# A bidirectional state-space scan taken over pairs of tokens, both directions in one step

## What is computed

```python
def ssm_direction(u_c, lam_re, lam_im, log_step, b_re, b_im, c_re, c_im, reverse):
    lam = lax.complex(lam_re, lam_im)
    step = jnp.exp(log_step)[:, None]
    lam_bar = jnp.exp(lam * step)
    b_bar = ((lam_bar - 1.0) / lam)[:, :, None] * b
    bu = jnp.einsum('blgh,gph->blgp', u_c, b_bar)
    a = jnp.broadcast_to(lam_bar, (1, bu.shape[1]) + lam_bar.shape)
    _, states = lax.associative_scan(_scan_combine, (a, bu), reverse=reverse, axis=1)
    return jnp.real(jnp.einsum('blgp,ghp->blgh', states, c))

y = u32 * d_skip + ssm_direction(forward) + ssm_direction(reverse)
y = jax.nn.gelu(y)
y = y * jax.nn.sigmoid(y @ w_glu + b_glu)
return rmsnorm(y, g_out)
```

## Time and profile before

| | |
|---|---|
| median of three runs | 1778.12 us (1773.86 to 1780.32) |
| the profiled execution | 1774.65 us, of which its span is 1772.8 us |
| PE busy | 1634.9 us, 92% of the span |
| DVE busy | 1386.7 us, 78% |
| ACT busy | 1069.4 us, 60% |
| POOL busy | 260.5 us, 15% |

### The profile page before, as it was taken

How to read it: one execution, slowest core, us unless ns; L and a number is a source line. 1 busy time by engine, 2 the same in 40 slices (tenths; PEclk the granted TensorE clock), 3 DMA queues, 4 the chain that set the end, 5 groups by cost and what they waited for, 6 DMA issues and landing times.

```text
span 1772.8 us, 21337 instructions
## 1 busy us (share of the span) xinstructions
PE 1634.9 (92%) x6878; PEld 1231.4 (69%) x6879; DVE 1386.7 (78%) x1421; ACT 1069.4 (60%) x1252; POOL 260.5 (15%) x202
## 2 busy tenths in 40 slices
PE   6978888999798888799999999999999999999994
PEld 5634346888673434588788788788788787887883
DVE  5699956444378996688888888888888888888883
ACT  4466624433245763477677677677676676776772
POOL 0666620000046655000000000000000000000000
PEclk9976699999997578899999999999999999999998
DMA  9210006455321000399899899899899798998980
GB/s 380 95 48 19 6 0 231 173 189 190 142 112 78 1 24 1 134 351 373 317 370 374 308 369 377 302 367 376 309 377 373 304 374 334 344 375 315 366 334 37
DMA packets 56927, 423.22 MB, mean 239 GB/s; under 512 B 6449, under 2 KB 6449, under 8 KB 7217
## 3 DMA queue, kind: packets, MB, share of 16 engines
q1 hardware_dynamic: 56016, 417.40, 61.6%
q0 software_dynamic: 864, 5.24, 0.7%
HBM read 421.57 MB, written 1.05 MB: 238 GB/s over the span
## 4 chain that ended last, share of the span: by engine, by line
PE 81%; DVE 9%; ACT 5%; issue 3%; POOL 1%; DVEq 0%; DMA 0%; ACTq 0%; SPq 0%; POOLq 0%
PE ps L1225 42%; PE ps L1213 20%; PE ps L1068 5%; PE ps L1082 2%; PE ps L1096 2%; PE ps L1317 2%; PE ps L1179 2%; PE ps L1164 2%; PE ps L1193 2%; DVE work L769 1%; DVE wl L822 1%; PE ps L1152 1%; PE ps L1140 1%; ACT wh L449 1%; DVE work L722 1%
## 5 line engine op out<-in xcount | busy, mean ns | idle before, releaser
L822 DVE TENSOR_TENSOR wl<-raw,wh 128x2048 fp32r<-128x2048 f32 x369 | 834.8, 2290 | 134.9 <-ACT wh L449 123.2
L449 ACT ACTIVATE wh<-raw 128x2048 fp32r<-128x2048 f32 x369 | 693.4, 1914 | 0.0
L1225 PE MATMUL ps<-wh,xh 128*128 128x512 f32 x1072 | 431.4, 402 | 9.4 <-DVE xl L909 5.5
L1225 PE MATMUL ps<-wl,xh 128*128 128x512 f32 x1072 | 419.5, 391 | 0.0
L1225 PE MATMUL ps<-wh,xl 128*128 128x512 f32 x1072 | 418.7, 391 | 0.0
L1225 PEld LDWEIGHTS ps<-wh,xh 128*128 128x128 f32 x1072 | 201.9, 188 | 50.0 <-issue 9.3
L1225 PEld LDWEIGHTS ps<-wl,xh 128*128 128x128 f32 x1072 | 201.7, 188 | 42.8
L1225 PEld LDWEIGHTS ps<-wh,xl 128*128 128x128 f32 x1072 | 202.3, 189 | 40.1 <-issue 1.7
L457 ACT ACTIVATE hidh<-ps 128x256 fp32r<-128x256 f32 (+1 forms) x123 | 49.5, 402 | 271.2 <-PE ps L1193 271.2
L1213 PE MATMUL ps<-wh,hidh 128*128 128x512 f32 x536 | 165.8, 391 | 5.8 <-DVE hidl L829 5.8
L1213 PE MATMUL ps<-wh,hidl 128*128 128x512 f32 x536 | 165.1, 389 | 0.0
(11 more groups left out here) (196 smaller groups left out, 1692.4 us busy)
## 6 DMA issues: line engine op xcount, KB each, us to landing
raw<-wffn SPq DMA_DIRECT2D x369, 1024.0 KB, 5.2
mixw<-wmix SPq DMA_DIRECT2D x12, 2048.0 KB, 8.1
bw<-bmat POOLq DMA_DIRECT2D x2, 1024.0 KB, 10.2
cat<-cmat POOLq DMA_DIRECT2D x2, 1024.0 KB, 14.9
qk<-wglu SPq DMA_DIRECT2D x2, 1024.0 KB, 4.8
X<-x_in SPq DMA_DIRECT2D x1, 1024.0 KB, 4.9
ybuf<-rows POOLq DMA_DIRECT2D x2, 512.0 KB, 3.5
y_out<-hn SPq DMA_DIRECT2D x2, 512.0 KB, 2.7
```

What stands on the lines that cost most here:

```text
L449: nc.scalar.activation(wh[:, slot], raw[:, slot], ACT.Copy).then_inc(s["hi_done"], 1)
L822: tt(wl[:, slot], raw[:, slot], wh[:, slot].bitcast(F32), ALU.subtract).then_inc(s["lo_done"], 1)
L1225: ins = mm(ps[:, b], x2[:, fx, t * P:(t + 1) * P], w2[:, slot, f * 512:(f + 1) * 512], start=(fx == 0 and i == 0), stop=(fx == KT - 1 and ...
```

## The change

The tokens are laid out by parity: partition p holds tokens 2p and 2p+1, so the 256 columns of a transposed tile are the 128 even tokens and then the 128 odd ones. The constants for distances in the attention follow that order. For the scan, tokens are taken in pairs. The recurrence over pairs has the squared transition (decay `small[:, 16]`, which is the exponential of twice the exponent; angles from twice the angle), 128 elements long instead of 256. Its input is b u(2k) and b u(2k+1), one of them multiplied by the transition, in one product of 64 rows. One step does the forward and the reverse direction of a pair of groups, 128 columns each, so there are 16 steps. Token outputs that the pair state doesn't hold are given by a local term: a 128x128 matrix `loc` for each two steps, which also holds the skip `d_skip`, times the pair of tokens.

What that takes on each engine:

- SP: `spread_u` copies `u` from `uT` into the pair layouts `ush` and `usw`, 8 + 8 DMAs in a layer between buffers of the core (each 32 partitions, 4 rows of 128 elements). `gather_y` copies the output of each of the four feature tiles back to the order of `glu`, 8 DMAs each (32 partitions of 128 elements). The last of them stands behind the loads of two 1 MB pieces, in whose buffers (`LENT`) the scan's temporaries now lie.
- POOL's queue: the matrix for b is 2 MB instead of 1 MB, that for c 2 MB instead of 1 MB, and `dmat` of 0.5 MB is new. The three operations of a step keep their shape; there are 16 of each in a layer instead of 32.
- DVE before step 0: `scalars` is rearranged (35 operations instead of 30); `turn_b` is new (12 operations of 128x512 elements); `fold_c` has six of 128x2048.
- PE before step 0: 32 transposes of 128x128 for b, which ACT empties in eight copies of 128x512. PE waits with `bu(0)` for them and for `ush`.
- DVE in a step: `fracs`, `rotate_in` and `add_in` keep their shape, the scan is four instructions of 128 elements instead of two of 256. Once in a layer, four operations of 32x256 add into `loc`.
- ACT in a step: four angle instructions of 128 elements instead of two of 256; the rest keeps its shape.
- PE in a step: `bu` is four products of 128 columns instead of two of 256, `outputs` too, and in every second step a product with `loc` of 128 columns. `local` is 32 products of 64 columns in a layer.
- The attention's stages stand two steps apart instead of four, and the six projections in steps 0 to 3. Half of `attention_out` now comes after the last scan.

```diff
-ZQKV_AT = (0, 1, 2, 4, 6, 8)
-HEAD_AT = [9 + 4 * h for h in range(HEADS)]
+ZQKV_AT = (0, 0, 1, 1, 2, 3)
+LOCAL_AT = 0
+HEAD_AT = [3 + 2 * h for h in range(HEADS)]
 ATN_AT = [HEAD_AT[2 * b + 1] + 6 for b in range(HEADS // 2)]
 T_EXP, T_PROBS, T_TURN, T_OUT = 2, 3, 4, 5
+STEPS = GP + 3
...
+        lent = raw[:, LENT[0]:LENT[-1] + 1].rearrange("p b n -> p (b n)")
...
+        yq = uT
+        ush = sb("ush", [P, PAIRS, NCH + 1])
+        usw = sb("usw", [P, PAIRS, NCH])
...
+            def spread_u(l):
+                sp.wait_ge(s["u_zero"], l + 1)
+                sp.wait_ge(s["emptied_act"], emptied(unit(l, "zu", 1))[1])
+                for q in range(4):
+                    for j in range(2):
+                        to = 64 * (q % 2) + 32 * j
+                        sp.dma_start(ush[to:to + 32, q // 2:PAIRS:2, j:j + NCH],
+                                     uT[32 * q:32 * q + 32, :, j * NCH:(j + 1) * NCH]).then_inc(s["in_ush"], 16)
...
+            def gather_y(l, ft):
+                sp.wait_ge(s["g_ready"], FT * l + ft + 1)
...
+                for b in range(2):
+                    for a in range(2):
+                        for j in range(2):
+                            at, to = 64 * a + 32 * j, 32 * (2 * b + a)
+                            sp.dma_start(yq[to:to + 32, ft, j * NCH:(j + 1) * NCH],
+                                         th[at:at + 32, ft, b * NCH:(b + 1) * NCH]).then_inc(s["in_yq_last" if ft == FT - 1 else "in_yq"], 16)
+            def mixer(l, k0, returned):
+                for k in range(k0, 6):
+                    mix(l, k)
+                    if k == 2:
+                        spread_u(l)
+                gather_y(l, 0)
+                glu(l)
+                for ft in range(1, FT - 1):
+                    gather_y(l, ft)
+                sp.wait_ge(s["c_done"], GP * (l + 1))
+                for slot, index in returned:
+                    load(slot, index, None)
+                gather_y(l, FT - 1)
...
-                pool.dma_start(bw[:], bmat[l]).then_inc(s["in_b"], 16)
-                pool.dma_start(craw[:], cmat[l]).then_inc(s["in_c"], 16)
...
+                pool.dma_start(cyt[:], bmat[l]).then_inc(s["in_b"], 16)
+                pool.dma_start(cw[:], cmat[l]).then_inc(s["in_c"], 16)
+                pool.dma_start(loc[:], dmat[l]).then_inc(s["in_d"], 16)
...
+                for d in range(2):
+                    turn = small[:, 4, 2 * i + d:2 * i + d + 1]
+                    c = slice(d * NCH, (d + 1) * NCH)
+                    nc.scalar.activation(phase[:, 0, c], cst[:, C_T:C_T + NCH], ACT.Copy, scale=turn)
+                    ins = nc.scalar.activation(phase[:, 1, c], cst[:, C_T:C_T + NCH], ACT.Identity, bias=col[:, 17:18],
+                                               scale=turn)
...
+                for k in range(PAIRS):
+                    u = unit(l, "bt", k)
+                    full(u)
+                    nc.scalar.activation(bw[:, k], ps[:, bank(u)].rearrange("p (r d m) -> p r d m", r=2, d=2),
+                                         ACT.Copy).then_inc(s["emptied_act"], 1)
...
+                for r in range(2):
+                    for d in range(2):
+                        ins = tt(btmp[:, r, d], b(r, d), lam(10, d), ALU.mult)
+                link(ins)
+                for r in range(2):
+                    for d in range(2):
+                        ins = tt(b(r, d), b(r, d), lam(9, d), ALU.mult)
+                link(ins)
+                for d in range(2):
+                    tt(b(0, d), b(0, d), btmp[:, 1, d], ALU.subtract)
+                    ins = tt(b(1, d), b(1, d), btmp[:, 0, d], ALU.add)
+                ins.then_inc(s["lamb_ready"], 1)
...
+                tt(ctmp[:, 0], c[0], f(1), ALU.mult)
+                link(tt(ctmp[:, 1], c[1], f(1), ALU.mult))
+                tt(c[0], c[0], f(0), ALU.mult)
+                link(tt(c[1], c[1], f(0), ALU.mult))
+                tt(c[0], c[0], ctmp[:, 1], ALU.subtract)
+                stt(c[1], c[1], -1.0, ctmp[:, 0], ALU.mult, ALU.subtract).then_inc(s["cw_ready"], 1)
...
-                stt(y, uT[:, ft], par[:, l, Q_D + ft:Q_D + ft + 1], ps[:, 2 + ft % 2, 0:SEQ],
-                    ALU.mult, ALU.add).then_inc(s["y_read"], 1)
-                dve.wait_ge(s["y_read"], FT * l + ft + 1)
-                link(tt(th[:, ft], y, y, ALU.mult))
+                dve.wait_ge(s["c_done"], GP * l + 4 * (ft + 1))
+                y = ps[:, 2 + ft % 2, 0:SEQ]
+                link(nc.vector.tensor_copy(yt[:, ft], y))
+                link(tt(th[:, ft], yt[:, ft], y, ALU.mult))
...
-                decay = small[:, 3, i:i + 1].to_broadcast([P, SEQ])
-                for r in range(2):
-                    ins = nc.vector.tensor_tensor_scan(st[:, n % 3, r], decay, ps[:, i % 2, r * SEQ:(r + 1) * SEQ], 0.0,
-                                                       ALU.mult, ALU.add)
...
+                    decay = small[:, 16, 2 * i + d:2 * i + d + 1].to_broadcast([P, NCH])
+                    for r in range(2):
+                        c = r * SEQ + d * NCH
+                        ins = nc.vector.tensor_tensor_scan(st[:, n % 3, r, d * NCH:(d + 1) * NCH], decay,
+                                                           ps[:, i % 2, c:c + NCH], 0.0, ALU.mult, ALU.add)
...
+            def turn_b(l):
+                pe.wait_ge(s["lamb_ready"], l + 1)
+                for k in range(PAIRS):
+                    u = unit(l, "bt", k)
+                    free(u)
+                    for r in range(2):
+                        for d in range(2):
+                            at = (2 * r + d) * P
+                            ins = nc.tensor.transpose(ps[:, bank(u), at:at + P], bt[:, k, r, d], ident)
+                    ins.then_inc(s["unit_done"], 1)
...
-                gp, d = i // 2, i % 2
-                ft, q = gp // 4, 32 * (gp % 4)
-                u = uT[q:q + 32, ft, ::-1] if d else uT[q:q + 32, ft, :]
-                for r in range(2):
-                    ins = mm(ps[:, i % 2, r * 256:r * 256 + 256], bw[q:q + 32, ft, d, r, :], u, start=True, stop=True,
-                             tile_position=(q, 0))
...
+                k, q = i // 2, 64 * (i % 2)
+                for d in range(2):
+                    u = ush[q:q + 64, k, NCH:0:-1] if d else ush[q:q + 64, k, 0:NCH]
+                    for r in range(2):
+                        c = r * SEQ + d * NCH
+                        ins = mm(ps[:, i % 2, c:c + NCH], bw[q:q + 64, k, r, d, :], u, start=True, stop=True,
+                                 tile_position=(q, 0))
...
+            def local(l, d):
+                u = unit(l, f"loc{d}")
+                free(u)
+                c = cw[:].rearrange("p r (k a d) (j n) -> p r k a d j n", a=2, d=2, j=2)
+                for k in range(PAIRS):
+                    for r in range(2):
+                        ins = mm(ps[:, bank(u), k * 64:k * 64 + 64], bt[:, k, r, d], c[:, r, k, :, d, d, :],
+                                 start=(r == 0), stop=(r == 1))
...
+                if i % 2 == 0:
+                    mm(ps[:, 2 + ft % 2, c:c + NCH], loc[:, k, :], usw[:, k, :], start=True, stop=False)
...
+                for d in range(2):
+                    for r in range(2):
+                        a = ro[:, i % 2, 0, r, d * NCH:(d + 1) * NCH]
+                        if d:
+                            a = a[:, ::-1]
+                        ins = mm(ps[q:q + 64, 2 + ft % 2, c:c + NCH], cw[:, r, 2 * i + d, :], a, start=False,
+                                 stop=(d == 1 and r == 1), tile_position=(0, q))
...
+                turn_b(l)
+                empty_wait(unit(l, "bt", PAIRS - 1))
+                pe.wait_ge(s["in_ush"], 128 * (l + 1))
                 bu(l, 0)
...
+                    if i == LOCAL_AT + 1:
+                        empty_wait(unit(l, "loc1"))
+                        pe.wait_ge(s["in_usw"], 128 * (l + 1))
+                    if 0 < i <= GP:
...
+                pe.wait_ge(s["in_yq"], 128 * (FT - 1) * (l + 1))
                 glu(l, 0, range(FT - 1))
-                outputs(l, ST - 1)
                 glu(l, 1, range(FT - 1))
-                pe.wait_ge(s["g_ready"], FT * (l + 1))
+                pe.wait_ge(s["in_yq_last"], 128 * (l + 1))
```

342 lines of the change are left out of this document (194 added, 148 removed).

## The result

The changed kernel takes **1742.22 us** (median of 4 runs, 1741.26 to 1744.0) against 1777.18 for the one before (4 runs): ratio 0.9814, 95% interval 0.9801 to 0.9827, so 35 us faster by the medians and 31 to 35 us by the interval. The forecast was 1717, its range 1693 to 1750. The profiled execution took 1741.26 us, its span is 1739.5.

A forecast was written before the change was run, and what follows sets the result against it. PE sets the pace in a mixer's first stage, then DVE. Gains of 40.6 and 38.8 us in the two layers, less 18 at their ends, give 61 us off 1774.65, hence 1717 us; range 1693 to 1750.

The forecast's parts named there:

- some waiting more: Allowance in the 8-in-10 range of 1693 to 1750 us for more waits than the forecast's own case.
- rival A: DVE's scans: an instruction of 128 elements takes as long as one of 256, 0.59 us; 1739 us, chance 8%.
- rival C: Steps 4 to 15: PE records cost the same whatever their columns, so PE takes over; 1797 us, chance 5%.
- What stands before `zu`: Start of a layer, up to the end of `zu`: the forecast put no cost on it.
- That is 3.7 us behind the `fracs` of the odd step ... some 0.6 us with the handoff, four times: Steps 5 to 15: ACT's rounding after a head's exponentials makes DVE's next `fracs` wait 0.6 us, four times.
- Before `bu(0)`: Before step 0: `turn_b`, transposes and copies of `u` meet at about 42.5 us, so `bu(0)` starts 9 us later.
- rival B: SP's copies are slow, at 1.43 us an issue: 23 us more in both layers, 1740 us, chance 14%.
- The end of the steps: From the last scan on: `gelu_in` at +6.5, `glu` group to +16.3, 3 us for next products; 9 us more a layer.
- As before: Steps 0 to 3 on PE: the projections, 192 records at 0.22, take 42.2 us, unchanged.
- Rival D: Nothing is lost: the waits (12 us) and the clock's share of the end (6 us) don't come; 1699 us, chance 11%.

The follow-up runs named there:

- e6: Changed kernel plus three scans of 128 elements more in each step, into a spare buffer that nothing reads: 1757.46 us.
- e7: Changed kernel with four of eight `ush` copies and four of the last eight `gather_y` copies issued from POOL's queue instead of SP's: 1744.88 us.
- e3: Changed kernel with POOL's loads for c and `loc` issued only after the first chunk of `mixw`: 1740.81 us.
- e1: Changed kernel with a head's transposes ahead of the next `bu` on PE: 1722.33 us.
- e2: Changed kernel with a head's exponentials ahead of the copy of the other head's transposes on ACT: 1728.87 us.
- e4: Changed kernel with the last outputs ahead of the second `atn` group on PE, and the last `gelu_in` ahead of half of `attention_out`: 1739.26 us.
- e5: Changed kernel with SP's copies of `u` issued ahead of the third chunk of `mixw`: 1734.96 us.
- e8: Changed kernel with the two projections for v moved from steps 2 and 3 to steps 4 and 6: 1725.33 us.
- c3: Changed kernel with the edits of e1, e2, e3, e4 and e5, plus the last `gelu_out` directly behind its `gelu_in`: 1704.54 us.
- c2: c3 plus the two projections for v in steps 4 and 6, as in e8: 1685.52 us.

## Why the prediction was right in sign and 25 us too hopeful

The time lies inside the range, on its slow side, but not for a reason that the forecast or a rival had priced. The prediction names as a sign of being wrong that the chain in steps 5 to 15 runs through PE or ACT rather than DVE. It does so at the five waits: DVE is busy 77% there, not 95%, and the last scan ends 165.7 us behind `zu`, not 159. Between the waits DVE's own work stays on the chain (e6). That the time still fell into the range is what the "some waiting more" in the range allowed for, not the mechanism.

**Right.** The scans (1.35 forecast, 1.27 measured from start to start) keep rival A out. The Trainium skill (VectorE: DVE Perf Modes, "The TRN2 errata") would have had two more scans cost 0.25 us; four start 1.27 apart in a step where two started 1.18 apart, so the trace shows 0.09. PE's records (0.136, forecast 0.16) keep rival C out. From `bu(0)` to the end of the scan of step 4 were 64.6 us forecast (42.5 to 107.1) and 64.2 measured (51.09 to 115.28). The last copies are 6.26 against 6.2 in all, by luck: eight issues took 4.95, 0.62 each in place of 0.50, and landing 1.8 in place of 2.7. The 2.0 us that the prediction takes from the Trainium skill (DMA: Bandwidth & Descriptors, "Anatomy of one DMA") is stated there for DMAs issued from GpSimd, while these go out on SP: 1.8 us here, and 4.5 from POOL in e7. The feed-forward blocks gave nothing back.

**Wrong, term by term, for layer 0.** The terms add to what is missing: 31.6 forecast, less 7.6 before the end of `zu`, less 6.6 from there to the last scan (165.7 against 159.1), less 3.6 at the end of the steps: 13.8, measured 13.6.

- *What stands before `zu`: costed at nothing, 7.6 us.* The forecast listed POOL's larger loads and priced none. Their 2.5 MB more hold back the first chunk of `mixw` (to 23.65), which starts `zu` 5.4 us late; e3 shows 3.5 us of it. The other 2.2 us are in the length of `zu`: its first ten records fill the 4 us from 24 to 28, where 20 did before. The profile of e1, whose `zu` starts at the same 23.93, gives a granted clock of 0.50 there, but that of the changed kernel lists 1.00, and its length differs between executions of the same code (15.52 to 16.96 in e1, e2, e4 and e5). How it arises is open.
- *"That is 3.7 us behind the `fracs` of the odd step ... some 0.6 us with the handoff, four times".* In mechanism this step failed most. It counted ACT's work from the exponentials on, as if they started when they could. They stand behind a copy, and that behind PE's transposes, `bu` and the scan. The waits are 15.8 us, not 2.4, and e1 and e2 take most of them away by order alone. In the sum it shows as 6 us: the stage took 90.6 us (115.28 to 205.91) against 78.6 + 6. Of those 6 the waits for ACT were 2.4; no row gave the rest, which was put down for a late PE. DVE's own work was 74.8, not 78.6, in part because a late `fracs` no longer runs beside POOL and takes 0.69 in place of 1.16.
- *Before `bu(0)`: 10.8 against 9.9.* Right in size by luck. The transposes took 3.66 us for 32, half of the 6.8 forecast: the granted clock is 1.00 there, and it was 0.50 to 0.67 in the row that gave the price; the copies took 10.0 from first issue (40.96 to 50.95), where 0.50 an issue and 2.7 to landing gave 6.7. The issues took 0.59 to 1.15, at a mean of 0.74: above the 0.50 taken, and half of rival B's 1.43. What ended last was the landing behind the chunk of `mixw`, which e5 shows and which the forecast had seen and thought covered.
- *The end of the steps: 22.5 against 18.9.* To the Tanh the terms gave 16.3; 3 us more were put on the products behind it. `gelu_in` came at +11.6, not +6.5. The order of PE was seen (the last outputs behind two groups of `atn`), but the eight `atn` records at the lower clock (5.15 us) were not counted. `glu` took 2.0 in place of 1.0. In return, the 3 us put on the products behind it did not come: from the Tanh to the first dense product are 31.25 us, 31.15 before. The row that they rest on was read too strictly: behind the gap of 3.10 us the four products took 1.53, between full and half speed, and the 2.07 stand behind the next gap.

In layer 1 the first term is absent, and the second is 7.0. The end took 22.7 us from the last scan to the Tanh, but it had taken 11.2 before, not the 9.85 of layer 0, so it costs 2.5 more than forecast: 29.8 - 7.0 - 2.5 = 20.3, measured 20.4.

**Not asked at all.** "As before" for the projections was right on PE, but the forecast took their packing into steps 0 to 3 as given. DVE idles 27 us behind them in layer 0, and e8 shows that 17 us in two layers were to be had by leaving two of them later.

Rival D (1699, nothing lost) lies between c3 and c2: the time was there, but not with this order.
